# A hybrid block's delta-rule layers: two gate units moved in front of the inverses' transposes, and three sets of length sums done in column groups

## The reference

```python
def hybrid_mixer(h, ...):
    proj = h @ w_in                                   # qkv, z_a, a, b, cf_val, cf_glu, z_b, gates
    qkv = silu(depthwise_conv_centred(qkv, qkv_conv_w))        # 5 taps
    q = l2_normalize(q);  k = l2_normalize(k)         # t * rsqrt(sum(t * t, -1) + EPS), 4 heads of 128
    o = gated_delta_chunked(forward) + flip(gated_delta_chunked(backward))
    o = o * rsqrt(mean(o * o, -1) + EPS) * dn_norm_w  # the same kind of length, per head
    y_a = (o * silu(z_a)) @ w_dn_out
    u = depthwise_conv_centred(cf_val * sigmoid(cf_glu), cf_conv_w) + cf_conv_b   # 31 taps
    y_b = (silu(layer_norm(u)) * silu(z_b)) @ w_cf_out
    gate = sigmoid(gate_lg + gate_b)                  # 2 x 1024 columns
    return (gate[:, :, 0] * y_a + gate[:, :, 1] * y_b) @ w_out
```

## Time and profile before

| | us |
|---|---|
| median of 3 runs | 2185.73 (2185.45 to 2186.78) |
| the profiled execution, whole | 2181.29 |
| its span, first to last instruction | 2180.0 |
| TensorE busy in the span | 2076.5 (95%) |
| VectorE | 1257.8 (58%) |
| ScalarE | 883.5 (41%) |
| GpSimd | 888.4 (41%) |

### The profile page before, as it was taken

The page is one execution under the profiler, slowest core; times in us unless marked ns, Lnnn a source line. Parts: engine busy times, 40 slices in busy tenths (PEclk is TensorE's granted clock), DMA queues, the critical chain, the costliest instruction groups (busy, mean ns, idle before and its releaser), DMA issues.

```text
span 2180.0 us, 26667 instructions
## 1 busy us (share of the span) xinstructions
PE 2076.5 (95%) x10724; PEld 1656.2 (76%) x10724; DVE 1257.8 (58%) x1944; ACT 883.5 (41%) x1413; POOL 888.4 (41%) x431
## 2 busy tenths in 40 slices
PE   8999999998999999999999999799999999899997
PEld 7888888675666788888887787678778787778775
DVE  5422223757677533222225979898653779898643
ACT  4222233323444543222235385344533475343632
POOL 4444443332113344444444553343334464343342
PEclk9999999999999999999999999999999999999998
DMA  4333333221001232333333222101222322011222
GB/s 154 110 135 97 97 97 106 96 70 39 30 30 49 75 96 91 97 97 97 97 98 94 68 78 69 38 30 29 79 87 87 95 80 69 28 30 40 78 87 78
DMA packets 46186, 169.09 MB, mean 78 GB/s; under 512 B 5232, under 2 KB 6000, under 8 KB 45808
## 3 DMA queue, kind: packets, MB, share of 16 engines
q1 hardware_dynamic: 45344, 165.60, 24.4%
q10 hardware_dynamic: 720, 1.79, 0.2%
HBM read 165.27 MB, written 2.10 MB: 77 GB/s over the span
## 4 chain that ended last, share of the span: by engine, by line
PE 78%; DVE 15%; ACT 6%; issue 1%; POOL 0%; DMA 0%; DVEq 0%; ACTq 0%
PE ps L384 22%; PE ps L386 21%; PE ps L385 21%; PE ps L440 2%; DVE blk_t L1927 1%; DVE outer L1925 1%; DVE cu L1825 1%; PE ps L633 1%; PE ps L617 1%; PE ps L602 1%; ACT dl L1424 1%; ACT whi L987 1%; PE ps L937 1%; DVE dl L2034 1%; PE ps L948 1%
## 5 line engine op out<-in xcount | busy, mean ns | idle before, releaser
L2154 POOL TENSOR_TENSOR wlo<-raw,whi 128x1024 fp32r<-128x1024 f32 x300 | 734.4, 2454 | 904.5 <-ACT whi L987 904.0
L384 PE MATMUL ps<-xh,whi 128*128 128x512 f32 x1584 | 645.4, 407 | 15.1 <-ACT gates L1162 6.2
L386 PE MATMUL ps<-xh,wlo 128*128 128x512 f32 x1584 | 620.4, 392 | 0.0
L385 PE MATMUL ps<-xl,whi 128*128 128x512 f32 x1584 | 619.9, 391 | 0.0
L384 PEld LDWEIGHTS ps<-xh,whi 128*128 128x128 f32 x1584 | 299.3, 189 | 102.1 <-issue 33.4
L987 ACT CAST whi<-raw 128x1024 fp32r<-128x1024 f32 x300 | 312.5, 1044 | 156.2 <-DMA raw<-in_stream 156.0
L385 PEld LDWEIGHTS ps<-xl,whi 128*128 128x128 f32 x1584 | 299.5, 189 | 63.0 <-issue 6.3
L386 PEld LDWEIGHTS ps<-xh,wlo 128*128 128x128 f32 x1584 | 298.9, 189 | 63.9
L1825 DVE SCALAR_TENSOR_TENSOR cu<-up,lcols,cu 128x512 f32<-128x512 f32 x180 | 182.0, 1063 | 0.1
L2190 POOL TENSOR_TENSOR cu<-cu,prod 128x512 f32<-128x512 f32 x60 | 87.6, 1459 | 149.0 <-ACT prod L1229 147.8
L1531 DVE TENSOR_TENSOR ml<-mid,mh 128x512 fp32r<-128x512 f32 x42 | 56.2, 1343 | 152.8 <-ACT mh L1048 152.8
(11 more groups left out here) (354 smaller groups left out, 3048.0 us busy)
## 6 DMA issues: line engine op xcount, KB each, us to landing
raw<-in_stream SPq DMA_DIRECT2D x300, 512.0 KB, 3.6
w1k<-in_w SPq DMA_DIRECT2D x1, 2048.0 KB, 8.1
w1v<-in_w SPq DMA_DIRECT2D x1, 2048.0 KB, 8.0
outT<-h SPq DMA_DIRECT2D x4, 512.0 KB, 2.7
h<-in_xT ACTq DMA_DIRECT2D x2, 512.0 KB, 7.2
h<-in_xT SPq DMA_DIRECT2D x2, 512.0 KB, 7.6
mats<-in_mats ACTq DMA_DIRECT2D x1, 448.0 KB, 10.4
msk<-in_masks SPq DMA_DIRECT2D x1, 258.0 KB, 3.8
```

Of the source, the lines that this page charges most:

```text
L384: pe.matmul(out, wh, hi, start=first, stop=False)
L385: pe.matmul(out, wh, lo, start=False, stop=False)
L386: return pe.matmul(out, wl, hi, start=False, stop=last)
L2154: pool.tensor_tensor(m.wlo[:, slot, :], m.raw[:, slot, :], m.whi[:, slot, :].bitcast(F32), ALU.subtract).then_inc(s.wlo)
```

## The change

Three things change, in both layers.

- LEAD_UNITS goes from 6 to 8 and FIRST_PRODUCTS from 2 to 3. Ten gate units are left for the delta rule before, eight after. Its slots hold 64 tiles, so none is left behind the last chunk; before, two units (16 tiles) were.
- The four separate sums of a set become `four_sums`: four float32 matmuls with an all-ones matrix of 32 columns, each to its own 32 partitions of one PSUM bank. ScalarE then does one Ln and one Exp for all four (`inverse_lengths`, into the new buffer `roots`), where it did four of each. `spread` brings each row back to 128 partitions of its own bank: four matmuls with 32 rows, whose weight is one column of `spot` (a one in the first of 32 rows) repeated 128 times.
- The sets move a little. In the conv stage the sums of the keys come together after j = 5 and the spreading after j = 6, ScalarE's part in front of the silu of j = 5. For the queries the sums come after the first gate unit, the spreading after the second. In the tail the sums come after the second z unit, the spreading after the third.

```diff
-LEAD_UNITS = 6
+LEAD_UNITS = 8
 GATE_UNITS = 16
 
-FIRST_PRODUCTS = 2
+FIRST_PRODUCTS = 3
...
+    def four_sums(out, rows):
+
+        for r in range(4):
+            ins = pe.matmul(out[32 * r:32 * r + 32], mat(m, "ones")[:, 0:32], rows[:, r, :], start=True, stop=True)
+        ins.then_inc(s.len_sum)
+
+    def spread(count, where):
+
+        pe.wait_ge(s.len_root, count)
+        for r, bank in enumerate(where):
+            one = mat(m, "spot")[32 * r:32 * r + 32, 0:1].broadcast_to([32, P])
+            ins = pe.matmul(ps[:, bank, :], one, m.roots[32 * r:32 * r + 32, :], start=True, stop=True)
+        ins.then_inc(s.spread)
...
-            if 2 <= j < 6:
-
-                pe.wait_ge(s.sq_qkv, 8 * l + j - 1)
-                if j == 5:
-                    pe.wait_ge(s.ab_read, l + 1)
-                    pe.wait_ge(s.decay, l + 1)
-                sum_rows(ps[:, (6, 7, 5, 4)[j - 2], :], [m.rt[:, j - 2, :]]).then_inc(s.sums_qkv)
+            if j == 5:
+                pe.wait_ge(s.sq_qkv, 8 * l + 4)
+                four_sums(ps[:, 6, :], m.rt)
+            if j == 6:
+                pe.wait_ge(s.ab_read, l + 1)
+                pe.wait_ge(s.decay, l + 1)
+                spread(3 * l + 1, (6, 7, 5, 4))
...
             if n == 0:
-                pe.wait_ge(s.l2, 8 * l + 4)
-                for r in range(4):
-
-                    pe.wait_ge(s.sq_qkv, 8 * l + 5 + r)
-                    pe.wait_ge(s.qconv, 12 * l + 9 + r)
-                    sum_rows(ps[:, r, :], [m.sqq[:, r, :]]).then_inc(s.sums_qkv)
+                pe.wait_ge(s.sq_qkv, 8 * l + 8)
+                pe.wait_ge(s.qconv, 12 * l + 9)
+                four_sums(ps[:, 0, :], m.sqq)
+            if n == 1:
+                pe.wait_ge(s.qconv, 12 * l + 12)
+                spread(3 * l + 2, range(4))
...
         z_unit(1)
-        for c in range(4):
-            pe.wait_ge(s.o_sq, 4 * l + c + 1)
-            sum_rows(ps[:, c, :], [m.rt[:, c, :]]).then_inc(s.o_sums)
+        pe.wait_ge(s.o_sq, 4 * l + 4)
+        four_sums(ps[:, 0, :], m.rt)
         z_unit(2)
+        spread(3 * l + 3, range(4))
         z_unit(3)
...
+        def inverse_lengths(count, bank, scale):
+
+            act.wait_ge(s.len_sum, count)
+            then(act.activation(ps[:, bank, :], ps[:, bank, :], ACT.Ln, bias=eps, scale=scale))
+            act.activation(m.roots[:], ps[:, bank, :], ACT.Exp, scale=-0.5).then_inc(s.len_root)
...
-            dve.wait_ge(s.root_qkv, 8 * l + n + 1)
+            dve.wait_ge(s.spread, 3 * l + 1 + n // 4)
...
-            dve.wait_ge(s.o_root, 4 * l + c + 1)
+            dve.wait_ge(s.spread, 3 * l + 3)
```

More of the change, by code:

```diff
@@ L168 @@
 SIGNALS = (
-    "wlo nl_even nl_odd unit xl xh whi eps in_par total sums even_squares g_scaled u_scaled ml down rope vtok "
-    "xr rot vxr vturn blk z1 in_w1v in_mix cmp1 hidden kc2 cmp2 kc_raw kc_rot kcc vc_raw gate_row cmask expd "
-    "score probs pt0 pt1 ptc turned o_new pv cw cturn vcc gts cscore ysum mix_lo h_new yl up wab_lo ab qconv "
-    "ab_raw ab_t sq_qkv ab_read decay sums_qkv gl l2 cum d_kk kk_read picked d_pre d_min filled o_sq o_sums "
-    "conv shared mean cu_sq var o_dn d_snew d_vns d_onew d_t d_u d_att d_ys d_qd d_at d_y d_qk d_us d_uy d_ttk "
-    "d_ttv d_kd d_s0 d_ks d_rest d_vn d_s d_q d_o act_step raw0 raw1 raw2 raw3 in_h0 in_h1 in_h2 in_h3 square "
-    "root scaled2 sil mid mh angle trig poly tanh gts_sig negmax csub cexp mix_hi gate_scaled sg yh prod "
-    "glu_sig y nh zero qkv root_qkv soft_dve soft_act cum_s d_dec cum_d z_used o_root cu_c root_cu cu_n "
+    "wlo nl_even nl_odd unit xl xh whi eps len_sum len_root spread in_par total sums even_squares g_scaled "
+    "u_scaled ml down rope vtok xr rot vxr vturn blk z1 in_w1v in_mix cmp1 hidden kc2 cmp2 kc_raw kc_rot kcc "
+    "vc_raw gate_row cmask expd score probs pt0 pt1 ptc turned o_new pv cw cturn vcc gts cscore ysum mix_lo "
+    "h_new yl up wab_lo ab qconv ab_raw ab_t sq_qkv ab_read decay gl l2 cum d_kk kk_read picked d_pre d_min "
+    "filled o_sq conv shared mean cu_sq var o_dn d_snew d_vns d_onew d_t d_u d_att d_ys d_qd d_at d_y d_qk "
+    "d_us d_uy d_ttk d_ttv d_kd d_s0 d_ks d_rest d_vn d_s d_q d_o act_step raw0 raw1 raw2 raw3 in_h0 in_h1 "
+    "in_h2 in_h3 square root scaled2 sil mid mh angle trig poly tanh gts_sig negmax csub cexp mix_hi "
+    "gate_scaled sg yh prod glu_sig y nh zero qkv soft_dve soft_act cum_s d_dec cum_d z_used cu_c root_cu cu_n "
     "cu_silu d_vt dve_step rms in_pos h_scaled d_t0 h_out out_dma "
@@ L1268, in qkv_silu @@
                 act.activation(sq, m.qkv[:, QKV_ORDER[j], :], ACT.Square).then_inc(s.sq_qkv)
-        def l2_roots(first, where):
-            for n, bank in enumerate(where):
-                act.wait_ge(s.sums_qkv, 8 * l + first + n + 1)
-                t = step(act.activation(ps[:, bank, :], ps[:, bank, :], ACT.Ln, bias=eps))
-            act.wait_ge(s.act_step, t)
-            for n, bank in enumerate(where):
-                act.activation(ps[:, bank, :], ps[:, bank, :], ACT.Exp, scale=-0.5).then_inc(s.root_qkv)
+        def inverse_lengths(count, bank, scale):
+            act.wait_ge(s.len_sum, count)
+            then(act.activation(ps[:, bank, :], ps[:, bank, :], ACT.Ln, bias=eps, scale=scale))
+            act.activation(m.roots[:], ps[:, bank, :], ACT.Exp, scale=-0.5).then_inc(s.len_root)
         def diagonal_blocks(t, bank):
@@ L1351, in layer @@
         z_unit(1)
-        for c in range(4):
-            act.wait_ge(s.o_sums, 4 * l + c + 1)
-            then(act.activation(ps[:, c, :], ps[:, c, :], ACT.Ln, bias=eps, scale=1.0 / P))
-        for c in range(4):
-            act.activation(ps[:, c, :], ps[:, c, :], ACT.Exp, scale=-0.5).then_inc(s.o_root)
+        inverse_lengths(3 * l + 3, 0, 1.0 / P)
         z_unit(2)
```

7 lines of the change are left out of this document (4 added, 3 removed).

## The result

The changed kernel took 2156.31 us (median of 4 runs, 2155.03 to 2159.35) against 2185.59 us before: a ratio of 0.9875, 95% interval 0.9862 to 0.9889, or 29.3 us less. The forecast was 19.8 us less. Direction and rough size were right. The two halves of the sum were both mis-sized, in opposite directions, so the nearness of the total is in part luck.

A forecast was written before the change was run, and what follows sets the result against it. TensorE was taken as the bound, busy 2076.5 of 2180.0 us, with its 10.0 us wait for VectorE's elimination the largest. Front 7.0 plus tail 2.9 us a layer, twice, gave 19.8 us less: 2165.9 us, range 2156 to 2178.

The forecast's parts named there:

- Part 1: Front: two gate units moved into TensorE's wait at the inverses' transposes; gain 7.0 us a layer, between 4 and 8.5.
- The place of the first products: Front, first products now behind the third gate unit: claimed to cost nothing, since ScalarE's sigmoid comes as before.
- The return of the clock to 1.00: Behind the transposes' wait: the 1.6 us wait left is too short to cool the clock, 1.9 us a layer gained.
- Part 2: Sums and spreading in narrow groups: 1.3 us a group if four products overlap, a set 2.6 us for 3.44.
- the rivals with half or no packing: Narrow groups overlap only partly (about 2171 us, chance 0.14) or not at all, 3.9 us a group (2180, chance 0.08).
- the slow one: Narrow groups run one after another at 1.2 GHz, 7.3 us a group: slower than before, 2216 us, chance 0.03.
- Part 3: Tail: VectorE's taps come last, five low parts stretching them, and TensorE waits 7.0 us; gain 2.9 us a layer.
- the sign of being wrong: Tail: TensorE waiting less than 4 us at the mean would show the tail forecast wrong.
- My own timetable for TensorE: Tail: without two units and with the cheaper set, TensorE reaches the mean at 1547.6 instead of 1559.37.
- The rival of the cheaper tail: Tail: clock stays up and only four taps are stretched, 2 x 4.05 us more gain, 2158 us; chance 0.06.
- that of the late inverses: Front: GpSimd meets the elimination at worse moments, inverses no earlier than 1375, gain 1 to 3 us, 2176; chance 0.05.

The follow-up runs named there:

- e1: Kernel before with eight leading units and three first products, its own sums kept (no column groups): 2163.37 us, ratio 0.9902.
- e2: Changed kernel with six leading units and two first products again, so only the column groups are new: 2177.68 us, ratio 0.9967.
- e6: Changed kernel with 35 (first layer) and 18 (second layer) tiny ScalarE copies ahead of the cast for the tail's second low part: 2173.79 us.
- e3: Changed kernel with the four unit-length scalings of VectorE one elimination step earlier (step 7 instead of 8): 2157.58 us.
- e5: Changed kernel with three (first layer) and four (second layer) small ScalarE copies ahead of the cast for the tail's third low part: 2156.80 us.
- e10: Changed kernel run once more, unaltered, beside later runs: 2157.69 us.
- e4: Changed kernel with one (first layer) and two (second layer) small ScalarE copies ahead of the cast for the tail's third low part: 2159.41 us.

## Why the prediction was right or wrong

- **What bounds the kernel.** Right: the wait at the inverses is set by VectorE's elimination, and the elimination by what GpSimd does beside it. But I then booked the gain at the wrong place. e1 shows that filling the wait brings the inverses hardly forward (0.5 us): what the two units give back, they give back where they stood before.
- **Part 1, forecast 7.0 us a layer, measured 2.6.** L908 started 129.92 us behind the conv start instead of the forecast 1371.3 - 1244.56 = 126.7, so 3.2 us late. The low part of unit 4, which I had placed beside the scalings that read PSUM, came before them and stretched an operation: the elimination ended 1.9 us later than forecast. The placing behind it took 5.07 us and not 4.15, as the last low part and the copies ran beside it: 0.9. The predicated copies beside the products are the rest: the first transposes came 1.7 us behind their start and not 1.4, and those of the second direction had to wait another 1.03 us, which I had not reckoned with. The place of the first products, which I had put at nothing, cost TensorE 0.84 us of waiting for ScalarE's sigmoid (0.50 before), but not on the path, since VectorE came last. The return of the clock to 1.00 was right in this profile, though the same waits brought it to 0.50 in others, so that was partly luck. It is worth little (0.6 us for my 1.9), since the split stands in its place: from L893 to the first 64x64 products 4.99 us before, 4.36 now.
- **Part 2, forecast 1.3 us a group, measured about 1.2 and 1.3.** Right, and the rivals with half or no packing are out, the slow one with them. Most of what I had booked in part 1, under the title of the two units, is what the groups bring by way of VectorE: 3.3 us in front by themselves (e2).
- **Part 3, forecast 2.9 us a layer, measured 11.2.** I let five low parts into the taps, and two got in. The failing step is "ScalarE now gets to the casts earlier, so five low parts fall into them". The third cast came later, not earlier, since ScalarE's work for the lengths now stands in front of it, and I took from the earlier trace rows that every low part that comes while VectorE runs is granted at the next boundary of an operation, as all of before were. The third came 6.82 us behind the second and was held off for the rest of the row. The mean waited 0.5 us where I had set 4 us as the sign of being wrong. The second layer of e6, with five granted, measured 6.84 us for my 7.0, and a clock that fell. Without that wait TensorE's own work sets nearly all of the tail: 37.60 - 26.42 = 11.2, that is 10.9 for the two units and 0.8 for the cheaper set, less the 0.5 us of waiting. My own timetable for TensorE had this gain (1559.37 - 1547.6 = 11.8; the 10.9 that I set beside the taps leaves the cheaper set out), and I rejected it.
- **The sum.** 4.4 too much in front and 8.3 too little behind give 13.8 instead of 9.9 a layer. The result lies inside the range (2156 to 2178), at its lower edge. The rival of the cheaper tail, 2158, came nearest and named the right place, but with four stretched taps and 7 us a layer of the 11.2; that of the late inverses held beside it. I had priced each of them alone, never both at once. That the total came within 10 us is owed to two errors of opposite sign.

## What to carry to other kernels

Work that is moved into a wait shortens nothing at the wait: ask what it leaves behind at the place where it stood, and whether anything else sets the end there. Where two engines share a way to memory, place the one's short stretches of work beside operations of the other that don't contend (here those that read PSUM, and, but for 0.2 to 0.3 us each, the transposes), by a semaphore if need be: two marks around 4 us of GpSimd work were worth some 3 to 6 us. And count a stretched operation by where it falls: a neighbour's 2.4 us operation costs a 0.2 us one its whole length. If the neighbour is the one held off, the row loses nothing, but whoever waits for the neighbour pays (TensorE 6.33 us in the first layer of e6).

## What the runs showed of the hardware

- A GpSimd subtraction beside a row of VectorE operations that follow each other without a gap (30 taps, one each 0.665 us) can be held off for the rest of the row: 10.54 us in the changed kernel, 14.45 us in e6. In the rows of taps it was held off in all 21 layers in which VectorE had run 6.2 us or more undisturbed, and never with up to 4.8 us. In the elimination, whose operations stand 0.03 us apart, it never was. The Trainium skill (SBUF — State Buffer, Who interferes with whom) says that VectorE operations with two SBUF inputs contend with GpSimd operations that read SBUF, that operations with at most one such input, outside VectorE's two-port modes, do not, and, of those modes, that whoever issues first keeps the shared pair for its whole instruction. The stretched taps and elimination operations agree (2.9 us instead of 0.67, 2.4 instead of 0.35), and so do the scalings that read PSUM (four took 2.48 us beside a low part in e3, and 2.48 us without one in the changed kernel). The transposes, with one input, took 2.1 to 2.2 us instead of 1.9. That GpSimd stays shut out while one VectorE operation follows the next, over some 12 taps in the changed kernel and 18 in e6, goes beyond the length of one instruction, and there the measurement decides.
- Four fp32 products of 32 columns and 512 elements that share all 128 rows hold TensorE for 0.99 us, four of 32 rows for 1.07.
- Two waits of TensorE of 1.9 and 1.0 us, 1.7 us apart, left the granted clock at 1.00 in both layers of the changed kernel, e5 and e10, in the first of e4 and the second of e6, and brought it to 0.50 in both layers of e1 and e3 and in the second of e4. These waits alone do not settle it, and neither does the kernel. Waits of 5.2, 6.8 and 10.0 us brought it to 0.50 each time.
